# A two-block transformer on one Trainium2 core: the last unit's expert pieces dealt over three more steps

## The reference

```
act = gelu(einsum('td,ted->te', tb, expert_u[eb]))
out = einsum('te,ted->td', gb * act, expert_v[eb])
```

```
gate, up = split(hf @ w_gate_up[l])
h_res = h_res + (silu(gate) * up) @ w_down[l]
```

## Time and profile before

| | us |
|---|---|
| median of 3 runs | 2488.56 |
| lowest and highest of them | 2484.80, 2490.49 |
| the profiled execution | 2485.22 |
| its span, first to last instruction | 2483.4 |
| TensorE busy | 2165.2 (87%) |
| VectorE busy | 1576.9 (63%) |
| DMA engines, mean rate over the span | 363 GB/s |

### The profile page before, as it was taken

The page is one execution under the profiler, slowest core; times in us unless marked ns, Lnnn a source line. Parts: engine busy times, 40 slices in busy tenths (PEclk is TensorE's granted clock), DMA queues, the critical chain, the costliest instruction groups (busy, mean ns, idle before and its releaser), DMA issues.

```text
span 2483.4 us, 40088 instructions
## 1 busy us (share of the span) xinstructions
PE 2165.2 (87%) x16356; PEld 2006.1 (81%) x16356; DVE 1576.9 (63%) x4201; ACT 457.4 (18%) x984; POOL 632.3 (25%) x518
## 2 busy tenths in 40 slices
PE   9998899777889978688986788887887799999999
PEld 7887689777779868677986776877867798899799
DVE  1258688686777868869777689885788533312310
ACT  2210232101123011113301132100231012101100
POOL 0023334333334333334333223332133200000000
PEclk9999899989989979899998898989989899999999
DMA  8589999999999999999999977999979969468474
GB/s 330 186 372 422 421 421 418 422 421 419 422 414 417 422 411 421 418 423 411 392 421 418 420 310 312 415 422 403 371 293 403 423 227 387 174 242 314 167 256 154
DMA packets 106917, 900.95 MB, mean 363 GB/s; under 512 B 12748, under 2 KB 16880, under 8 KB 17904
## 3 DMA queue, kind: packets, MB, share of 16 engines
q0 software_dynamic: 73904, 537.43, 52.9%
q1 hardware_dynamic: 31728, 357.95, 36.4%
q10 hardware_dynamic: 1104, 3.02, 0.3%
HBM read 897.30 MB, written 1.05 MB: 362 GB/s over the span
## 4 chain that ended last, share of the span: by engine, by line
PE 39%; DMA 36%; DVE 18%; issue 4%; POOL 2%; ACT 1%; SPq 0%; DVEq 0%; POOLq 0%; ACTq 0%
DMA row<-in_experts,idx 20%; PE ea L956 11%; PE pa L956 10%; DMA more<-in_experts,idx 8%; DMA wring<-in_weights 8%; DVE row L1972 5%; DVE acc L1955 3%; PE ea L874 2%; PE pa L676 2%; PE pa L782 2%; POOL row L2388 1%; DVE topi L1864 1%; PE pa L829 1%; PE ea L964 1%; DVE topv L1860 1%
## 5 line engine op out<-in xcount | busy, mean ns | idle before, releaser
L2388 POOL DMA_INDIRECT row<-in_experts,idx x448 | 556.8, 1243 | 1198.7 <-DVE acc L1955 559.1
L1972 DVE CUSTOM_DVE_ANT_0 row<-row,h2n 128x1024 f32<-128x1024 f32 x448 | 534.9, 1221 | 187.4 <-DMA row<-in_experts,idx 186.5
L874 PE MATMUL ea<-diag,row 128*128 128x128 f32 x3808 | 497.7, 296 | 139.1 <-DVE diag L1994 139.1
L874 PEld LDWEIGHTS ea<-diag,row 128*128 128x128 f32 x3808 | 486.3, 211 | 152.1 <-DVE diag L1994 150.6
L1955 DVE SCALAR_TENSOR_TENSOR acc<-row,wgt,acc 128x1024 f32<-128x1024 f32 x207 | 265.1, 1281 | 2.0
L1464 ACT ACTIVATE gl<-dots 128x4 f32<-128x4 f32 x128 | 26.3, 206 | 945.1 <-DVE dots L1972 945.0
L956 PE MATMUL ea<-hB,wring 128*128 128x144 f32 (+1 forms) x1056 | 147.7, 304 | 20.9 <-DMA wring<-in_weights 20.9
L956 PEld LDWEIGHTS ea<-hB,wring 128*128 128x128 f32 x1056 | 144.0, 208 | 23.3 <-DMA wring<-in_weights 22.8
L956 PE MATMUL pa<-hB,wring 128*128 128x144 f32 (+1 forms) x1056 | 137.6, 291 | 17.6 <-DMA wring<-in_weights 15.0
L956 PEld LDWEIGHTS pa<-hB,wring 128*128 128x128 f32 x1056 | 133.9, 197 | 21.0 <-DMA wring<-in_weights 16.2
L782 PE MATMUL pa<-hA,wring 128*128 128x128 f32 x960 | 123.1, 281 | 0.0
(11 more groups left out here) (540 smaller groups left out, 3245.6 us busy)
## 6 DMA issues: line engine op xcount, KB each, us to landing
wring<-in_weights SPq DMA_DIRECT2D x110, 2048.0 KB, 12.0
wlate<-in_weights SPq DMA_DIRECT2D x25, 2048.0 KB, 8.3
wring<-in_weights SPq DMA_DIRECT2D x22, 1408.0 KB, 6.8
wlate<-in_weights SPq DMA_DIRECT2D x10, 1408.0 KB, 6.5
more<-in_weights SPq DMA_DIRECT2D x5, 2048.0 KB, 8.1
row<-in_experts,idx POOLq DMA_INDIRECT x448, 19.0
row<-in_weights SPq DMA_DIRECT2D x3, 2048.0 KB, 16.6
wring<-in_weights SPq DMA_DIRECT2D x3, 1792.0 KB, 11.1
```

The costliest lines, as they stand in the source:

```text
L874: m = pe.matmul(EA[c // 4][:, (c % 4) * P:(c % 4 + 1) * P], v[:, c * P:(c + 1) * P], diag[:, DIAG_SLOTS * (q % 2) + i, :], start=False, st ...
L1972: dve.tensor_tensor_reduce(out=r, in0=r, in1=h2n[:, u % 2, :], scale=1.0, scalar=0.0, op0=ALU.mult, op1=ALU.add, accum_out=dots[:, g % 2, ...
L2388: pool.indirect_dma_start(out=expert_rows[slot], out_offset=None, in_=table, in_offset=bass.IndirectOffsetOnAxis(ap=idx[:, k % 2, GB * g + ...
```

## The change

The pieces are dealt over three more steps of unit 1, its first three down products. The last sums now stand ahead of `dn3` and the closing call ahead of `dn4`. Step 1 of unit 2 moves from ahead of `dn4` to ahead of `dn7`.

```
-EARLY = (4,)
+EARLY = (7,)
+OVER = 3
...
 def last_order():
 
-    beside = [0] * STEPS2 + [1] * (STEPS2 - KC)
-    share = SHARE2 + SHARE2[:STEPS2 - KC]
+    beside = [0] * STEPS2 + [1] * (STEPS2 - KC + OVER)
+    share = SHARE2 + SHARE2[:STEPS2 - KC + OVER]
     pieces = (PAIRS * GROUPS - 1) * TURN
...
-    for c in range(KC):
-        if c < 2:
+    for c in range(OVER, KC):
+        if c < OVER + 2:
             out.append("rows")
         if c in EARLY:
             out.append(2)
```

## The result

The changed kernel takes 2494.53 us (22 runs, 2489.72 to 2499.44), the kernel before 2488.09 us on the same chips (22 runs). The ratio is 1.0027, interval 1.0018 to 1.0035: 6.4 us slower, where 5.3 us faster was forecast. The profiled execution took 2491.67 us, with a span of 2489.9 us from its first to its last instruction.

What follows compares the result with a forecast made beforehand. VectorE bounds attention, DMA the feed-forward stretches with gathers, TensorE everything from 1990 us on. 2485.2 us profiled minus 5.3 won at the gathers' end, other terms 0, gives 2479.9, or 2483.2 as a median of runs; range 2476 to 2491.

Steps and rivals of the forecast that it cites:

- at step 24 we are 10 us ahead: Unit 1's feed-forward start: eight pieces fewer done by then, at 1.25 us each, make the layer 10 us earlier.
- the first rival: Attention stretches: engine round trips set them, so removing pieces does not shorten them; 1.0 us slower, chance 0.20.
- bounds of -6 and +5.3: Heavy pieces picking experts, shifted against the attention's score waits: 6 us won to 5.3 us lost, taken as 0.
- the two ways: End of unit 1's gathers: gain 6.5 us counting bytes, 4.0 us by the loop of two buffers; middle 5.3 taken.
- the bound of 1.8 us: Unit 1's downs: weight waits of 0.87 us at every second down cost 1.8 us at most; 0 taken.
- the latest time foreseen: Last gather's issue, with TensorE in unit 1's step 33: expected at 1981 to 1987 us.
- The second rival: Unit 1's downs with pieces: weight waits move there and matmuls run at half clock; 10.3 us slower, chance 0.12.

Runs made afterwards that it cites:

- the tail alone: Kernel before, its deal kept through unit 1's step 23 (199 pieces done), the other 49 over steps 24 to 37 with the changed closing order: 2484.38 against 2488.75 us.
- the kernel with heavier downs: Pieces dealt over five downs, with more of the last ones there (232 done at `dn0`): 2487.64 against 2488.31 us for the kernel before, 0.9991.
- five downs: The tail alone with its pieces reaching over five downs of unit 1 instead of three: 2482.16 against 2487.09 us for the kernel before, 0.9980.

## Why the prediction was wrong

**The step that failed.** "A piece that moves from a stretch bound by VectorE to one bound by DMA wins nothing by itself: the first 10 us (8 x 1.25) come back", and with it "at step 24 we are 10 us ahead". Lengths in us, means over the traces that share a deal in the stretch (before: six traces, in unit 1's attention five; changed: four, two of them with the two or three pieces moved at the units' edge):

```
                                pieces       before's deal  changed deal
unit 0, steps 1 to 23           62 -> 60         160.2          156.3
unit 0, gate and up products    50 -> 48         108.2          108.8
unit 0, downs                   24 -> 23          61.8           66.6
unit 1, steps 1 to 23           63 -> 60         155.0          155.9
sum                            199 -> 191        485.2          487.6
```

The head was to be 10 us shorter and is 2.4 us longer. Single traces of one deal differ by up to 7 us in the sum, so it can't be told from unchanged, but it is not 10 us shorter. In its idle time TensorE has lost nothing and won nothing: 79.1 instead of 78.3 us; the other 1.5 us are busy time at a lower clock. The medians agree: from the tail alone (-4.4) to the changed kernel (+6.4) are 10.8 us. In the traces they are these 2.4 us and, from unit 1's first gate product to unit 2, the step from 153.0 to 160.0 us (mean of six traces with 191 pieces at step 22). So the eight pieces had to be paid in the tail, at 0.9 us each, and nothing came back for them in the head.

- *Five of the eight pieces leave the attention stretches, and there a piece pays 0.3 to 0.4 us, not 1.25.* The two kernels that thin one attention stretch show it. What misled me is in the earlier trace rows: 92% busy VectorE in windows inside the stretches. Over the whole stretch VectorE is busy 135.0 of 159.5 us and TensorE 135.2; neither bounds it alone. My reading is that a shorter VectorE queue only helps where VectorE is the last to be ready: TensorE's waits for it, listed above, fell by 1.8 us for 9.9 us less of work. That is the first rival, to which I gave 0.20. I priced it at 1.0 us slower because I still credited the other three pieces.
- *The other three pay 0.8 to 1.0 us each where the stretch is DMA's, but in the changed kernel they bring nothing.* By measured prices its head should be about 5 x 0.3 + 3 x 0.9 = 4.2 us shorter (an estimate). Of the 6.6 us to the 2.4 measured, 4.8 are the longer downs of unit 0: 3.0 us more of TensorE waiting (14.9 against 12.0) and 1.8 us more of it busy at a lower clock. Places seem to matter there, since a kernel with nearly the same pieces in them has 65.05 us too. Which instruction in them costs it stays open: taking away the one wait that looked guilty (ScalarE's) changed the stretch by 0.7 us.
- *Pick blocks and groups shifted against the attention seem to cost or win 3 to 4 us.* I had bounds of -6 and +5.3 and took 0. The lengths don't show it in unit 1: 156.4, 157.7 and 157.8 us in the three kernels where everything stands one group later, against 153.2 to 159.0 in five traces with the deal of before. TensorE's idle time there does: 24.0 to 25.4 us against 19.0 to 23.3. In unit 0 the changed deal wins 3.9 us with two pieces less, and its four traces lie below all of the six. This is a difference between traces, and no experiment moved a pick block alone and won.

**What held, in part.** The tail: in the forecast's frame unit 1's gate and up products and downs were to take 10 - 5.3 = 4.7 us more than before with eight more pieces to do, and take 160.0 - 156.2 = 3.8 us more. Without those eight, in the tail alone, the gain is 4.4 us, near the two ways' 4.0 and 6.5. The traces alone would not carry this, since the kernel with only step 1 moved takes 160.0 us there too; the medians do. In the changed kernel's trace the downs with pieces, the last sums and step 1 of unit 2 cost 0 (50.42 us against 50.50), and unit 2's first loads go out at 2050.82, 13.9 us ahead of their first use. The seven other traces with pieces in three downs and this closing order have 51.6 to 52.7 us there, so that 1 or 2 us are the likelier price, inside the bound of 1.8 us or near it. The last gather came 8 us later than the latest time foreseen because the layer was 3.6 us later at unit 1's first gate product instead of 10 us ahead.

**The second rival** did not happen in the changed kernel, but the kernel with heavier downs shows what one such wait costs: behind a wait of 3.54 us the 44 matmuls of a down take 8.68 us instead of 5.66, as the earlier trace rows had it for the gate and up products.

## What to carry to other kernels

Before work is moved out of a stretch, read over the whole of it how much of each engine's time is waiting for the other: with VectorE and TensorE both at 85%, ten microseconds less for VectorE gave two or three. Background work should leave the stretch whose bound it shares (here DMA's, at 0.8 to 1.0 us a piece) and stay in the one where it is nearly free (0.3 to 0.4 us), which a deal in proportion to step sizes can't do. Try the end of a plan without its beginning: the tail alone won 4.4 us, the same tail behind an evenly thinned head lost 6.4. And before the lengths of one stretch are compared between two traces, split them into TensorE's busy and idle time: the clock alone moved one by 5.6 us.

## What the runs showed of the hardware

The same 640 matmuls ran at different clocks behind waits of nearly the same sum. In unit 1's gate and up products the kernel before waits for weights 17.7 us in all, of which 9.8 in two waits of 4.80 and 4.99 us, and the granted clock is 0.92. With five downs it waits 15.2 us in nine waits of 0.62 to 2.86 us, one a tile, and the granted clock is 1.00; it is 1.00 as well in the two other kernels with five downs and 199 pieces at step 22, whose longest waits there are 3.23 and 3.42 us. The 640 matmuls are busy 81.06 us instead of 88.03: 7.0 of the 9.4 us between the two stretches are clock, 2.5 are waits.

The length of a wait alone does not say what follows. With five downs the first 32 matmuls behind each of the nine waits took 4.19 us, and after 4.8 us in the kernel before they took 7.12 us. But in the kernel before they took 5.86 us after a wait of only 2.65 us:

```profile
1933.14 5.86 PE L956 MATMUL ea<-hB,wring 128*128 128x144 f32 x32 [2.65 <-DMA wring<-in_weights]
```

That short waits spread over the tiles keep the clock up is what these traces suggest; no run varied the spread alone.
